# Attention in a hybrid encoder block: one VectorE operation per unit, transposed powers, the division by their sum put after the value product

## The reference, cut to what matters

```python
def row(r):
    rs = jnp.clip(r - kh // 2, 0, rows - kh)
    ...
    s = jnp.einsum('bhmqd,bhimjd->bhmqij', qr, kr).astype(jnp.float32) + bias
    p = jax.nn.softmax(s.reshape(sh[0], sh[1], sh[2], sh[3], kh * NA_KB), axis=-1)
    o = jnp.einsum('bhmqij,bhimjd->bhmqd', p, vr)
...
s = jnp.einsum('thzd,znd->thzn', q, sub_keys)        # PEER: scores of the product keys
...                                                  # top 16 of each half, top 16 of their sums
act = jax.nn.gelu(jnp.einsum('thkd,td->thk', u[eidx], xc), approximate=False)
return jnp.einsum('thk,thkd->td', (gate * act), v[eidx])
```

## Time and profile before

| | |
|---|---|
| three runs | 4132.88, 4134.06, 4142.45 us, median 4134.06 us |
| span of the profiled execution | 4129.6 us, 4.5 us under the median of the runs |
| busy in the span | PE 2880.7 us (70%), DVE 2564.6 us (62%), ACT 822.4 us (20%), POOL 2104.8 us (51%) |
| DMA | 1396.14 MB, mean 338 GB/s |
| `u` and `v` gathers (software queue) | 1086.75 MB, 68.2% of the 16 DMA engines' span |
| attention, pass 0 | from about 733 to 843 us |
| attention, passes 1 to 3 | about 1283 to 1430, 2070 to 2237, 2885 to 3048 us |

### The profile page before, as it was taken

One profiled execution on the slowest core, in us unless ns is written; L12 is line 12 of the kernel. 1 busy time (PEld: TensorE's weight loads), 2 busy tenths in 40 slices (PEclk: granted clock), 3 DMA queues, 4 the chain that ended last, 5 costly groups with the idle time before them and its releaser, 6 DMA issues.

```text
span 4129.6 us, 39869 instructions
## 1 busy us (share of the span) xinstructions
PE 2880.7 (70%) x13083; PEld 1529.4 (37%) x13083; DVE 2564.6 (62%) x5345; ACT 822.4 (20%) x1841; POOL 2104.8 (51%) x2147
## 2 busy tenths in 40 slices
PE   5999998797866866886586767856857773333334
PEld 4887776543333522332343223323432230000000
DVE  4642446415788866547887665478876666766652
ACT  3323113411132410112233001122420010000000
POOL 1100304002576555556766565567665667777775
PEclk8999999998988988997788878987988886566656
DMA  7415764536999999999999999999999999999998
GB/s 216 69 54 161 223 194 153 169 127 231 374 407 393 388 399 405 403 402 394 389 399 399 404 406 398 405 387 392 398 395 404 407 403 407 395 409 404 399 409 350
DMA packets 507852, 1396.14 MB, mean 338 GB/s; under 512 B 65880, under 2 KB 136512, under 8 KB 506624
## 3 DMA queue, kind: packets, MB, share of 16 engines
q0 software_dynamic: 298768, 1086.75, 68.2%
q1 hardware_dynamic: 208880, 306.84, 21.4%
HBM read 1336.91 MB, written 56.51 MB: 337 GB/s over the span
## 4 chain that ended last, share of the span: by engine, by line
DMA 33%; DVE 12%; PE 11%; issue 10%; POOL 10%; ACT 0%; SPq 0%; DVEq 0%; POOLq 0%; ACTq 0%
DMA ring<-in_peer_u,idx 27%; PE ps_l L1649 6%; POOL ring L2248 5%; POOL ring L2241 5%; DVE junkF L2424 5%; DMA ring<-in_peer_v,idxT 4%; PE acc L2470 2%; DMA gin<-zg_scr 1%; PE ps_l L1718 1%; DVE nmax L1985 1%; DVE st L1971 1%; DMA lane<-n_scr 1%; DMA lane<-state_scr 0%; PE ps_l L1713 0%; PE ps_l L1699 0%
## 5 line engine op out<-in xcount | busy, mean ns | idle before, releaser
L2424 DVE CUSTOM_DVE_ANT_0 junkF<-ring,ps_n2F 128x1024 bf16<-128x1024 f32 x1024 | 1249.1, 1220 | 841.0 <-DMA ring<-in_peer_u,idx 745.4
L2248 POOL DMA_INDIRECT ring<-in_peer_u,idx x1024 | 1002.8, 979 | 1060.5 <-DVE dots L2424 644.2
L2470 PE MATMUL acc<-ring,spread 128*32 128x512 f32 x4096 | 716.6, 834 | 906.7 <-DMA ring<-in_peer_v,idxT 906.5
L2241 POOL DMA_INDIRECT ring<-in_peer_v,idxT x1024 | 989.1, 966 | 332.6 <-issue 298.5
L1649 PE MATMUL ps_l<-lane 128*128 128x512 f32 x1856 | 849.5, 612 | 44.5 <-issue 23.1
L2470 PEld LDWEIGHTS acc<-ring,spread 128*32 128x32 f32 x4096 | 145.1, 135 | 1347.6 <-issue 1344.2
L1649 PEld LDWEIGHTS ps_l<-lane 128*128 128x128 f32 x1856 | 354.8, 196 | 514.7 <-issue 508.9
L514 POOL DMA_DIRECT2D bias<-rpb_scr x16 | 13.2, 829 | 326.8 <-PE ps_dt L799 278.9
L1848 PE MATMUL ps_l<-lane 128*128 128x128 f32 (+1 forms) x832 | 138.7, 307 | 46.1 <-ACT lane L1890 46.1
L1896 ACT ACTIVATE st<-st,nmax 128x512 f32<-128x512 f32 x128 | 92.4, 722 | 386.2 <-DVE nmax L1985 386.0
L1848 PEld LDWEIGHTS ps_l<-lane 128*128 128x128 f32 (+1 forms) x832 | 111.5, 201 | 124.1 <-ACT lane L1890 102.9
(11 more groups left out here) (352 smaller groups left out, 4021.0 us busy)
## 6 DMA issues: line engine op xcount, KB each, us to landing
lane<-in_w_in SPq DMA_DIRECT2D x18, 2048.0 KB, 19.1
lane<-in_peer_wq SPq DMA_DIRECT2D x16, 2048.0 KB, 19.3
w_z<-in_w_in SPq DMA_DIRECT2D x16, 1024.0 KB, 5.9
adaB<-in_w_ada SPq DMA_DIRECT2D x16, 1024.0 KB, 6.2
lane<-in_w_na_br SPq DMA_DIRECT2D x8, 2048.0 KB, 19.0
lane<-in_w_ssd_br SPq DMA_DIRECT2D x8, 2048.0 KB, 19.8
lane<-in_w_out SPq DMA_DIRECT2D x8, 2048.0 KB, 19.3
ring<-in_peer_u,idx POOLq DMA_INDIRECT x1024
```

What stands on the lines that cost most here:

```text
L2241: pool.indirect_dma_start(v_rows[:, nv % RV, :], None, a["peer_v"][0], bass.IndirectOffsetOnAxis(ap=idxT[:, m % 2, col:col + 1], axis=0)). ...
L2248: pool.indirect_dma_start(u_rows[:, n % RU, :], None, a["peer_u"][0], bass.IndirectOffsetOnAxis(ap=idx[:, i % RI, j:j + 1], axis=0)).then_ ...
L2424: nc.vector.tensor_tensor_reduce(out=junk[:, :], in0=u_rows[:, n % RU, :], in1=ps_n[:, :], scale=1.0, scalar=0.0, op0=ALU.mult, op1=ALU.ad ...
L2470: last = nc.tensor.matmul(acc[q * QUAD:(q + 1) * QUAD, cols], spread[:, m % 2, c0:c0 + QUAD], v_rows[:, nv % RV, cols], start=(g == 0 and ...
```

## The change

The diff does five things.

1. Scores are made with their sign turned: the queries are stored times -1/8 (line 622), the bias is stored as mask minus bias, with a mask of +1e30. VectorE then adds bias to scores and takes the row minimum in one `tensor_tensor_reduce`, followed by a one-column read of its accumulator. The separate maximum (line 1985) is gone. ScalarE's exponential has scale -1.
2. `diag` and its VectorE operation are gone. The turn is now a TensorE transpose, four to each unit. For an odd unit ScalarE first puts the powers of the last 64 keys in front of the others (a second, 64-column exponential), so that the blocks lie whole; the buffer `probs` has 64 columns more for it.
3. The value product has its operands swapped: turned powers stationary, values moving. It gives queries by features of both heads, 128x128. ScalarE takes the two diagonal 64x64 pieces out of it and multiplies by the reciprocal of the sum (`raw`): the late normalisation.
4. Two new matmuls of 64x64 with the identity (`final_bank`) turn `raw` back into features by queries, both heads in one bank, and ScalarE moves them in one 128x64 operation (`keep_final`).
5. In pass 0 the turned powers are kept by VectorE; in passes 1 to 3 still by ScalarE. `PE_COST["att"]` falls from 0.58 to 0.45.

No DMA is added or removed.

```diff
@@ -498,10 +498,10 @@
-                    nc.gpsimd.affine_select(out=m[:, 0:edge], in_=m[:, 0:edge], compare_op=ALU.is_ge, fill=MASKED,
+                    nc.gpsimd.affine_select(out=m[:, 0:edge], in_=m[:, 0:edge], compare_op=ALU.is_ge, fill=-MASKED,
...
-                    nc.gpsimd.affine_select(out=m[:, NA_KW:], in_=m[:, NA_KW:], compare_op=ALU.is_ge, fill=MASKED,
+                    nc.gpsimd.affine_select(out=m[:, NA_KW:], in_=m[:, NA_KW:], compare_op=ALU.is_ge, fill=-MASKED,
@@ -518,8 +518,8 @@
-                    nc.gpsimd.tensor_tensor(bias[:, p % 2, :, :], bias[:, p % 2, :, :],
-                                            colmask[:, :].unsqueeze(1).broadcast_to([P, SLOTS, GRID_W]), ALU.add).then_inc(bias_done, 1)
+                    nc.gpsimd.tensor_tensor(bias[:, p % 2, :, :], colmask[:, :].unsqueeze(1).broadcast_to([P, SLOTS, GRID_W]),
+                                            bias[:, p % 2, :, :], ALU.subtract).then_inc(bias_done, 1)
@@ -619,7 +619,8 @@
-                    nc.scalar.activation(row[:, b % 2, :], ps_x[b % 2][:, :], ACT.Copy).then_inc(q_row, 1)
+                    nc.scalar.activation(row[:, b % 2, :], ps_x[b % 2][:, :], ACT.Copy,
+                                         scale=-(HEADDIM ** -0.5) if b < KD else 1.0).then_inc(q_row, 1)
@@ -1183,14 +1184,16 @@
-        st = sb("st", [P, RS, HALF])
+        st_room = sb("st", [P, RS * (GRID_W + HALF)])
+        st = st_room[:, 0:RS * HALF].rearrange("p (r n) -> p r n", r=RS)
+        probs = st_room[:, :].rearrange("p (r n) -> p r n", r=RS)
...
-        rinv = sb("rinv", [P, 2])
+        rinv = sb("rinv", [P, 4])
...
@@ -1674,6 +1679,12 @@
         def values_bank(a_pass, u):
             return ps_n[:, 0:P] if a_pass == 0 and u % 2 else ps_l[:, HALF:HALF + P]
 
+        def final_bank(a_pass, u):
+            return (ps_l[:, 2 * HALF:] if a_pass or u % 2 else acc[:, HALF:])[:, 0:HEADDIM]
...
@@ -1826,7 +1837,7 @@
         def pe_attend(pe, n, part):
             a_pass, it = JOBS[n][1:]
...
@@ -1837,7 +1848,7 @@
                 p, i = divmod(u, nr)
                 pe.wait_ge(pt_ev, g0 + u + 1)
                 if u >= held:
-                    pe.wait_ge(o_done, g0 + u - held + 1)
+                    pe.wait_ge(raw_done, g0 + u - held + 1)
@@ -1845,56 +1856,83 @@
                 for j, (keys, b, tile) in enumerate(terms):
                     if odd and j == len(terms) - 1:
                         pe.wait_ge(half_done, odd_units(a_pass, u) + 1)
-                    last = nc.tensor.matmul(values_bank(a_pass, u), V[keys, p % RP, tile, :], PT[keys, u % 2, b, :], start=(j == 0), stop=(j == len(terms) - 1))
+                    last = nc.tensor.matmul(values_bank(a_pass, u), PT[keys, u % 2, b, :], V[keys, p % RP, tile, :], start=(j == 0), stop=(j == len(terms) - 1))
                     if odd and j == 0:
                         last.then_inc(half_done, 1)
                 last.then_inc(pv_done, 1)
+            u = it - 4
+            if part == 1 and 0 <= u < units:
+                pe.wait_ge(raw_done, g0 + u + 1)
+                for hh in range(2):
+                    last = nc.tensor.matmul(final_bank(a_pass, u)[side(hh), :], raw[:, u % 2, :], ident[:, side(hh)], start=True, stop=True)
+                last.then_inc(fin_mm, 1)
             u = it - 2
             if part == 2 and 0 <= u < units:
                 odd = (first_row[rows[u % nr]] - KEY0[a_pass]) % 2
                 pe.wait_ge(exp_done_a, g0 + u + 1)
-                pe.wait_ge(diag_done, g0 + u + 1)
                 if u >= held:
                     pe.wait_ge(pt_ev, g0 + u - held + 1)
+                if u > held:
+                    pe.wait_ge(o_done, g0 + u - held)
                 turned = turned_bank(a_pass, u)
-                for b in range(odd, 4):
-                    c0 = b * P - odd * GRID_W
-                    last = nc.tensor.matmul(turned[:, b * P:(b + 1) * P], st[:, u % RS, c0:c0 + P], diag[:, u % 2, :], start=True, stop=True)
-                if odd:
-                    nc.tensor.matmul(turned[GRID_W:, 0:P], st[:, u % RS, 0:GRID_W], diag[:, u % 2, :], start=True, stop=True)
-                    last = nc.tensor.matmul(turned[0:GRID_W, 0:P], st[:, u % RS, HALF - GRID_W:], diag[:, u % 2, :], start=True, stop=True)
+                for b in range(4):
+                    c0 = b * P + (0 if odd else GRID_W)
+                    last = nc.tensor.transpose(turned[:, b * P:(b + 1) * P], probs[:, u % RS, c0:c0 + P], ident[:, :])
                 last.then_inc(pt_mm, 1)
             if part == 2 and a_pass and it + 1 < units:
                 pe_scores(pe, a_pass, it + 1)
         def act_attend(act, n):
             a_pass, it = JOBS[n][1:]
...
-            u = it - 4
-            if u >= 0:
-                p, i = divmod(u, len(ROWS[a_pass]))
-                f = value_set[PASSES[a_pass][i // 2]]
-                act.wait_ge(pv_done, g0 + u + 1)
-                if p == 0 and i % 2 == 0 and f >= SETS:
-                    act.wait_ge(p_mm, number[set_last[f - SETS]] + 1)
-                for hh in range(2):
-                    part = slice(hh * HEADDIM, (hh + 1) * HEADDIM)
-                    last = nc.scalar.activation(inT[part, f % SETS, p, i % 2 * GRID_W:(i % 2 + 1) * GRID_W], values_bank(a_pass, u)[part, part], ACT.Copy)
-                last.then_inc(o_done, 1)
-            u = it - 3
-            if 0 <= u < units:
-                act.wait_ge(pt_mm, g0 + u + 1)
-                if u >= 2:
-                    act.wait_ge(pv_done, g0 + u - 1)
-                nc.scalar.activation(PT[:, u % 2, :, :], turned_bank(a_pass, u).rearrange("p (b n) -> p b n", b=4), ACT.Copy).then_inc(pt_ev, 1)
-            u = it
-            if u < units:
-                act.wait_ge(max_done, g0 + u + 1)
-                if u >= 4:
-                    act.wait_ge(rinv_done, g0 + u - 3)
-                nc.scalar.activation(st[:, u % RS, :], st[:, u % RS, :], ACT.Exp, bias=nmax[:, u % 2:u % 2 + 1],
-                                     accum_out=rsum[:, u % 4:u % 4 + 1]).then_inc(exp_done_a, 1)
+            def raw_values(u):
+                if 0 <= u < units:
+                    act.wait_ge(pv_done, g0 + u + 1)
+                    act.wait_ge(rinv_done, g0 + u + 1)
+                    if u >= 2:
+                        act.wait_ge(fin_mm, g0 + u - 1)
+                    for hh in range(2):
+                        last = nc.scalar.activation(raw[side(hh), u % 2, :], values_bank(a_pass, u)[side(hh), side(hh)], ACT.Copy,
+                                                    scale=rinv[side(hh), u % 4:u % 4 + 1])
+                    last.then_inc(raw_done, 1)
+
+            def keep_turned(u):
...
+            def keep_final(u):
+                if 0 <= u < units:
+                    p, i = divmod(u, len(ROWS[a_pass]))
+                    f = value_set[PASSES[a_pass][i // 2]]
+                    act.wait_ge(fin_mm, g0 + u + 1)
+                    if p == 0 and i % 2 == 0 and f >= SETS:
+                        act.wait_ge(p_mm, number[set_last[f - SETS]] + 1)
+                    nc.scalar.activation(inT[:, f % SETS, p, i % 2 * GRID_W:(i % 2 + 1) * GRID_W], final_bank(a_pass, u), ACT.Copy).then_inc(o_done, 1)
+
+            def powers(u):
...
+                    if (first_row[ROWS[a_pass][u % len(ROWS[a_pass])]] - KEY0[a_pass]) % 2:
+                        nc.scalar.activation(row[:, 0:GRID_W], row[:, HALF:], ACT.Exp, bias=least, scale=-1.0).then_inc(ends_done, 1)
+                        act.wait_ge(ends_done, odd_units(a_pass, u) + 1)
+                    nc.scalar.activation(row[:, GRID_W:], row[:, GRID_W:], ACT.Exp, bias=least, scale=-1.0,
+                                         accum_out=rsum[:, u % 4:u % 4 + 1]).then_inc(exp_done_a, 1)
+
+            raw_values(it - 4)
+            if a_pass == 0:
+                powers(it)
+                keep_final(it - 4)
+            else:
+                keep_turned(it - 3)
+                keep_final(it - 4)
+                powers(it)
@@ -1958,9 +1996,15 @@
         def dve_attend(v, n):
             a_pass, it = JOBS[n][1:]
...
             nr = len(rows)
+            u = it - 3
+            if a_pass == 0 and 0 <= u < units:
+                v.wait_ge(pt_mm, g0 + u + 1)
+                if u >= 2:
+                    v.wait_ge(pv_done, g0 + u - 1)
+                nc.vector.tensor_copy(PT[:, u % 2, :, :], turned_bank(a_pass, u).rearrange("p (b n) -> p b n", b=4)).then_inc(pt_ev, 1)
             u = it
...
@@ -1968,21 +2012,15 @@
-                nc.vector.scalar_tensor_tensor(out=st[:, u % RS, :], in0=scores_bank(a_pass, u), scalar=HEADDIM ** -0.5,
-                                               in1=bias[:, p % RP, s0:s0 + NA_KH, :].rearrange("p s c -> p (s c)"),
-                                               op0=ALU.mult, op1=ALU.add).then_inc(s_read, 1)
+                nc.vector.tensor_tensor_reduce(out=probs[:, u % RS, GRID_W:], in0=scores_bank(a_pass, u),
```

(16 more changed lines are left out.)

35 lines of the change are left out of this document (24 added, 11 removed).

## The result

The changed kernel takes 4161.12 us (4147.53 to 4164.99), the kernel before in the same comparison 4133.47 us: a ratio of 1.0051 (1.0035 to 1.0067). Run again it was 1.0064 (1.0049 to 1.0079). The ratios, with their 95% intervals, are not quotients of the two medians and differ from them by up to 0.0016, or 7 us; where the two tell different amounts both are given. Forecast were 4118 us, and faster. Its profiled execution was its fastest run (4147.53 us, span 4145.8).

A forecast was written before the change was run, and what follows sets the result against it. Full DMA engines bound the kernel from the first gathers on, TensorE in pass 0. Pass 0's -16 us and 0 for passes 1 to 3 took 4129.6 to 4114 us of span, plus 4.5 to the median: 4118 us, range 4104 to 4136.

The forecast's parts named there:

- Pass 0: First attention pass: unit 2.71 us, 0.535 less, over 29 full iterations 15.5 us; first three and last four at 0.
- The copy on VectorE: Pass 0: copy of turned powers, 0.69 us, lets the value product start 0.93 after the scores, not 0.86: +0.07.
- needed six iterations later, 16 us; the last of them lands in 4.1 us: Pass 0: SP's loads for a pair of heads have 16 us until needed; the last lands in 4.1 us.
- Clock in pass 0: Pass 0: clock expected to stay at 0.98; rival: falls to 1.2 GHz, unit 5.3 us, 4194 us, chance 0.03.
- I book 0: Passes 1 to 3: no net change booked, with ends of -7 and +36 us.
- shortfall of TensorE in packed slots: Passes 1 to 3: TensorE needs 135, 148, 135 us against slots of 123, 137, 134; 12, 11 and 1 short.
- about three slots or 10 us of lag: Passes 1 to 3: a `v` ring of 11 rows covers this lag; 0 to 4 us lost in passes 1 and 2 each.
- The recurrences get 5 or 6 slots more: up to 4 of their 7 us come back: SSD recurrences: 7 us lost at DMA share 0.99; VectorE's savings and extra slots return up to 4 us.
- the prediction's sign of being wrong: Passes 1 to 3: DMA shares under 1.00 at the end of attention stretches, with TensorE waiting on line 1914.
- The turn's wait: Passes 1 to 3: each turn waits 0.5 us for ScalarE to move the small products out, 16 us in all.
- the slow rival: Passes 1 to 3: TensorE falls behind, 66 us short, 30 in the rings, 36 starving gathers: 4154 us; chance 0.12.
- when TensorE is late, its waits for ScalarE vanish: Passes 1 to 3: argument that today's waits for ScalarE's copy, 13.9 us in pass 2, would not stay.

The follow-up runs named there:

- the late loads: Changed kernel, attention cost back at 0.58, merge weights and gates of pass 0 loaded behind the last head pair's operands: 4116.07 us, 0.9956 of the kernel before.
- the old table: Changed kernel with the attention cost in the slot assignment set back from 0.45 to 0.58: 4128.97 us, 0.9988 of the kernel before.
- The new table: Kernel before with only its attention cost set from 0.58 to 0.45: 4161.63 us, 1.0065; on the slow kind of chip 4311.24 us, 0.9958.

## Why the prediction was wrong, point by point

- **Pass 0: right in mechanism, short by a stall, and its size right in part by luck.** The unit is 2.79 us where 2.71 was said: values 1.09 (0.99), turn 0.50 (0.44), small products 0.26 (0.35), scores 0.95 (0.93). The copy on VectorE binds as said: it starts 0.20 behind the scores and the value product 0.06 behind its end. With the late loads the whole is 16.4 us, against 16 forecast, but two errors cancel in it: the full units gave 11.7 us where 15.5 stood, and the first ones, put at 0, gave 4.1. In the changed kernel it was 10.4, since the sentence that failed is "needed six iterations later, 16 us; the last of them lands in 4.1 us": that is the median of six landings, and the fourth pair's loads stand behind 13 us of other issues.
- **Clock in pass 0: right.** The granted clock was 1.00 there save in the first 4 us, as before, and for 3.4 us at the stall (0.96 over 105 us with it, 0.98 over 100 us without it). The transposes, 0.50 of 2.79 us, took nothing from it. The Trainium skill (TensorE: Matmul & The Clock Gate, Part 4: PE-mode transpose) says that a transpose doesn't count as busy the way a matmul does; the trace shows no effect of it here.
- **Passes 1 to 3, "I book 0": the failed step.** Measured were 30 us lost, 18 to 20 in the recurrences and 10 to 12 in the rest. The 0 was right for the attention's new form (3068.7 against 3069.4 us with the old table), wrong for the table. Two of its terms failed. The first: I had worked out a shortfall of TensorE in packed slots (12, 11 and 1 us) and covered it by the `v` ring, "about three slots or 10 us of lag", to 0 to 4 us each in passes 1 and 2. In pass 2 that holds (nothing lost); in pass 1 9 to 11 us were lost. The cover wasn't there: the lag goes through VectorE, which takes scores and dots in one order, and through the `u` ring of 5. A loss of 10.7 us stands in pass 1 of the kernel before with that table as well, without the new wait and with fewer waits for scores, so the new wait isn't its cause there. The second term is the larger one and has the next point.
- **"The recurrences get 5 or 6 slots more: up to 4 of their 7 us come back": wrong in sign.** They lost 18 to 20 us, two thirds of the whole. The prediction gave them more slots and asked nothing about their places. At the new places 14 to 17 of 24 steps of sixteen small matmuls ran at or near the low clock, behind idle stretches, where it had been 8 to 10, and VectorE waited 16 to 22 us more for them, in order. The share of the DMA engines fell there, from 1.03 at 397 GB/s to 0.97 at 358 in slots 80 to 112, and not at the end of the attention, where the prediction's sign of being wrong looked.
- **The turn's wait** of 0.5 us is there (0.41 each, 24 times, 10.0 us in slots 112 to 176) and is nothing by itself: with the old table it is the same 10.0 us, and nothing is lost. The old waits for ScalarE's copy stayed, as the slow rival supposed (17.1 us against 14.3): "when TensorE is late, its waits for ScalarE vanish" failed. That rival's 4154 us was nearest, but partly by luck: its place was right for a third of the loss (packed slots, in pass 1), its cause mostly wrong, since the kernel before loses the same by the table alone.
- **Sum.** -10 in pass 0 and +30 in the slots, where -16 and 0 stood. This is the profiled run, the fastest of its four; 1 to 8 us of the measured loss (21 and 26 by the ratios, 28 by the medians) are in neither.

## What to carry to other kernels

A planner's cost that is lowered because an engine's work got less still moves every job of the pass: price each region for itself, and test the table alone on the old kernel before crediting or blaming the new code. Stretches of slots are not jobs: when a plan moves work across a boundary, compare to the end of the pass before calling a stage slower. When a stage gets faster, look up what is queued ahead of its next operands and not the median landing time; the cover may have been the slowness. And before counting on a ring to cover a lag, look whether an engine between takes late work and the ring's work in one order.

## What the runs showed of the hardware that was not expected

- Chips differ: from 3500 to 4000 us the core's DMA moved 403 GB/s on one kind and 367 to 375 on the other (the 256 late slots took 667 and 719 to 731 us), and the kernel before took 4133 to 4139 and 4327 to 4353 us. The new table in the kernel before lost 27 us on the one and gained 19 us on the other.
- Sixteen 128x64 matmuls took 1.89 us in a row of work, at a granted clock of 1.00, and 3.51 us after 4.20 us of idle time, at 0.50.
- The issues of two weight loads and two gate loads took SyncE 6.26 and 7.07 us, and a load of 352 KB issued 5 us behind them landed 9 us after its issue, where the median was 4.1.
- A minimum over 512 PSUM columns in the operation that adds the bias took 0.69 us, the same as the addition alone before, with a read of 0.08 behind it.
